# Starting the moving operands of the rounded products 60 bytes into a group of 64 bytes, in a two-block transformer kernel

## What is computed

```python
for i in range(2):                                   # first block
    h = h + 0.5 * swiglu(rms_norm(h, g_ffn1[i]), ffn1_w_in[i], ffn1_w_out[i])   # 1024 -> 2*2816 -> 1024
    hn = rms_norm(h, g_mix[i])
    h = h + (mla_mixer(hn, ...) if i == 0 else fox_mixer(hn, ...))              # two kinds of attention
    h = h + 0.5 * swiglu(rms_norm(h, g_ffn2[i]), ffn2_w_in[i], ffn2_w_out[i])
    gate = sigmoid(rms_norm(h, g_ple[i]) @ ple_w_gate[i])
    h = h + gate * (p[i] @ ple_w_proj[i])
# second block
proj = rms_norm(x) @ w_in                            # 1024 -> 3592
x = x + concat([short_conv_mixer(...), gated_deltanet(...)]) @ w_out
x = x + hier_moe(rms_norm(x))                        # 32 experts, 2 of them per token, inner width 512
return rms_norm(x)
```

## Time and profile before

| | |
|---|---|
| time, median of 3 runs | 1735.52 us (1734.45 to 1735.61) |
| the profiled execution | 1735.63 us, of which the span from first to last instruction is 1733.8 us |
| TensorE busy | 94% of the span, 10376 matmuls |
| VectorE, ScalarE, GpSimd busy | 57%, 35%, 3% |
| mean granted TensorE clock | 0.987 |
| DMA | 415.65 MB, 240 GB/s over the span |

### The profile page before, as it was taken

One profiled execution on the slowest core, in us unless ns is written; L12 is line 12 of the kernel. 1 busy time (PEld: TensorE's weight loads), 2 busy tenths in 40 slices (PEclk: granted clock), 3 DMA queues, 4 the chain that ended last, 5 costly groups with the idle time before them and its releaser, 6 DMA issues.

```text
span 1733.8 us, 25871 instructions
## 1 busy us (share of the span) xinstructions
PE 1631.1 (94%) x10376; PEld 1300.8 (75%) x10376; DVE 987.8 (57%) x1660; ACT 611.2 (35%) x809; POOL 54.3 (3%) x82
## 2 busy tenths in 40 slices
PE   6999999999999999999999999999989788778877
PEld 6999857899998999888899999999854344334333
DVE  6787655687766877865487785788331111111112
ACT  5333346433335333365543334553421000000001
POOL 3000005000000000001200000000000000000000
PEclk9999999999999999999999999999989999999999
DMA  6555441454554455444155555332599999999996
GB/s 267 191 191 185 183 182 74 182 182 181 184 223 176 182 188 191 184 165 182 66 190 187 191 192 202 139 128 92 222 376 426 426 428 427 428 428 427 428 428 268
DMA packets 49240, 415.65 MB, mean 240 GB/s; under 512 B 5616, under 2 KB 5648, under 8 KB 7824
## 3 DMA queue, kind: packets, MB, share of 16 engines
q1 hardware_dynamic: 49104, 414.61, 60.7%
q10 hardware_dynamic: 64, 0.03, 0.0%
HBM read 413.54 MB, written 1.05 MB: 239 GB/s over the span
## 4 chain that ended last, share of the span: by engine, by line
PE 75%; DMA 18%; DVE 3%; ACT 2%; issue 1%; SPq 0%; POOL 0%; DVEq 0%; ACTq 0%
PE bank L546 67%; DMA sb_moe_ring<-experts 18%; PE bank L1240 6%; DVE sb_ring_lo L2001 1%; ACT sb_high L1514 1%; PE bank L735 0%; PE bank L824 0%; DMA sb_h<-xT 0%; SPq L471 0%; ACT sb_high_first L1514 0%; DVE sb_nmax L2134 0%; DVE sb_x_parts L2030 0%; ACT sb_expg L1614 0%; PE bank L944 0%; ACT L1471 0%
## 5 line engine op out<-in xcount | busy, mean ns | idle before, releaser
L2001 DVE TENSOR_TENSOR sb_ring_lo<-sb_ring,sb_high 128x2304 fp32r<-128x2304 f32 (+4 forms) x180 | 352.0, 1957 | 132.4 <-ACT sb_high L1514 131.9
L546 PE MATMUL bank<-sb_x_parts,sb_high 128*128 128x512 f32 (+1 forms) x1792 | 407.0, 366 | 0.2
L546 PEld LDWEIGHTS bank<-sb_x_parts,sb_high 128*128 128x128 f32 x1792 | 317.7, 189 | 49.3 <-DVE sb_ring_lo L2001 0.5
L1514 ACT ACTIVATE sb_high<-sb_ring 128x3072 fp32r<-128x3072 f32 x100 | 275.7, 2757 | 147.2 <-PE bank L546 119.6
L546 PE MATMUL bank<-sb_x_parts,sb_ring_lo 128*128 128x256 f32 x1632 | 257.9, 284 | 0.0
L546 PEld LDWEIGHTS bank<-sb_x_parts,sb_ring_lo 128*128 128x128 f32 x1632 | 228.5, 192 | 6.7
L546 PE MATMUL bank<-sb_act_hi,sb_ring_lo 128*128 128x256 f32 x704 | 199.2, 283 | 0.0
L546 PE MATMUL bank<-sb_act_hi,sb_high 128*128 128x256 f32 x680 | 192.6, 283 | 2.0 <-DVE sb_ring_lo L2001 1.5
L546 PE MATMUL bank<-sb_act_lo,sb_high 128*128 128x256 f32 x680 | 192.4, 283 | 0.0
L1240 PE MATMUL bank<-sb_moe_ring,sb_act 128*32 128x512 f32 x512 | 130.1, 655 | 41.2 <-DMA sb_moe_ring<-experts 41.1
L1556 ACT ACTIVATE sb_expg<-sb_gate_r 128x256 f32<-128x256 f32 x88 | 36.9, 419 | 339.3 <-DVE sb_gate_r L2064 339.2
(11 more groups left out here) (385 smaller groups left out, 1893.9 us busy)
## 6 DMA issues: line engine op xcount, KB each, us to landing
sb_ring<-weights SPq DMA_DIRECT2D x133, 1536.0 KB, 6.5
sb_moe_ring<-experts SPq DMA_DIRECT2D x185, 1024.0 KB, 21.1
sb_qk<-experts SPq DMA_DIRECT2D x4, 1024.0 KB, 15.0
sb_moe_ring<-experts SPq DMA_DIRECT2D x8, 256.0 KB, 17.2
sb_h<-xT SPq DMA_DIRECT2D x2, 512.0 KB, 7.7
sb_ring<-weights SPq DMA_DIRECT2D x2, 512.0 KB, 8.5
sb_oT<-experts SPq DMA_DIRECT2D x1, 1024.0 KB, 15.4
sb_pin<-pT SPq DMA_DIRECT2D x1, 512.0 KB, 18.1
```

The lines of the kernel that those rows point to most:

```text
L546: ins = nc.tensor.matmul(o, l, r, start=start, stop=stop, skip_group_check=True)
L1514: nc.scalar.activation(high_of(n)[:, lo * P:hi * P], ring[:, n % RING, lo * P:hi * P], ACT.Copy).then_inc(done, 1)
L2001: return V.tensor_tensor(ring_lo[:, n % RING, cols], ring[:, n % RING, cols], high_of(n)[:, cols].bitcast(F32), ALU.subtract)
```

## The change

The three tensors whose slices move through the array in rounded products get 16 elements (64 bytes) more, and the operands begin at element 15 of them, 60 bytes behind a multiple of 64. The operand's first group of 64 bytes then holds one element of it, and a run of 256 columns touches 17 groups instead of 16. `act` and `act_lo` share their place, so `act` is shifted alike. To keep the same things from overlapping, 16 elements stand behind `hn`, and several tensors are made in another order: `params` and the narrow columns (`gq`, `eps_col`, `peak`) stand first, `qk`, `v_tok` and `oT` ahead of `h`, `act_hi` behind `sq`. Every tensor other than the shifted views still begins at a multiple of 64 bytes (the narrow columns aside, which are columns of one tensor now).

Each engine has the same instructions in the same order as before; only addresses and strides differ. The shifted operands are moving ones in the rounded products named above. They are stationary ones in `fox_qkv` and at the gates (`x_parts`), and in the experts' down product (`act`). The written side moves too: ScalarE's `x_hi` and VectorE's `x_lo`, `act_hi`, `act_lo` and `act` are written to shifted places.

```diff
+LINE = 16
+INSIDE = 15
...
+        def inside(flat, shape):
+
+            n = math.prod(shape[1:])
+            names = "abc"[:len(shape) - 1]
+            dims = {a: shape[1 + i] for i, a in enumerate(names)}
+            return flat[:, INSIDE:INSIDE + n].rearrange(f"p ({' '.join(names)}) -> p {' '.join(names)}", **dims)
...
-        sb("below_ring", [P, 32])
+        params = sb("params", [P, NPAR])
+        narrow = sb("narrow", [P, 16])
+        gq, eps_col, peak = narrow[:, 0:4], narrow[:, 4:5], narrow[:, 5:6].bitcast(I32)
...
-        act_hi = sb("act_hi", [P, 2, T], F32R)
+        qk = sb("qk", [P, 2 * H, T])
+        qT, kT = qk[:, 0:H, :], qk[:, H:2 * H, :]
+        v_tok = sb("v_tok", [P, 2, D])
+        oT = sb("oT", [P, KD, T])
         h = sb("h", [P, KD, T])
-        x_parts = rounded_view("x_parts", [P, 2, KD, T])
+        x_parts = inside(rounded_view("x_parts", [P, 2 * KD * T + LINE]), [P, 2, KD, T])
         x_hi, x_lo = x_parts[:, 0, :, :], x_parts[:, 1, :, :]
         hn = sb("hn", [P, KD, T])
+        sb("behind_hn", [P, LINE])
         sq = sb("sq", [P, KD, T])
+        act_hi = inside(sb("act_hi", [P, 2 * T + LINE], F32R), [P, 2, T])
...
-        act_lo = rounded_view("act_lo", [P, 2, T])
-        act = sb("act", [P, 2, T])
...
+        act_lo = inside(rounded_view("act_lo", [P, 2 * T + LINE]), [P, 2, T])
+        act = inside(sb("act", [P, 2 * T + LINE]), [P, 2, T])
```

More of the change, by code:

```diff
@@ L7 @@
 from contextlib import ExitStack
+import math
 import numpy as np
@@ L262, in two_block_kernel @@
         route = sqh[:, :, :, :].rearrange("p a b t -> p (a b t)")[:, 0:2 * 352].rearrange("p (c n) -> p c n", c=2)
[L263 to L266, removed]
         posi = v_tok[:, 0, 0:2].bitcast(I32)
```

## The result

The changed kernel takes 1726.36 us (median of 6 runs, 1724.46 to 1727.27), the kernel before 1735.57 us beside it (6 runs, 1734.45 to 1736.29). The ratio is 0.9946, with a 95% interval of 0.9935 to 0.9956: 9.2 us less, a fifth of the 48.6 us of the forecast. The first rows are the page of the kernel after: busy time by engine, then the chain, against the earlier trace rows.

The account below looks back on a forecast made before the run. TensorE was taken as the bound up to about 1250 us, then the experts' transfers. Gains of 15.1 us (512 columns) and 33.5 us (256 columns), together 48.6, took 1735.6 to 1687.0 us; the range was 1672 to 1740 us.

Parts of the forecast that it names:

- What bounds the kernel: Whole kernel: TensorE bounds it up to about 1250 us, then the experts' transfers, whose start moves rigidly with TensorE.
- That 13.3 ns is a first group of 16 elements at half rate: Rounded matmuls: the 13.3 ns beyond their columns is the first 64-byte group arriving at 0.83 ns per element.
- 512 columns, -10.7 ns each, -15.1 us: 1408 rounded matmuls with shifted moving operands: 226.7 to 216.0 ns each, 15.1 us less.
- 256 columns, -8 ns each, -33.5 us: 4192 rounded matmuls with shifted moving operands: about 8 of the 10.7 ns can be had, 33.5 us less.
- The floor of the weights' load, 112 ns: 256-column rounded matmuls: weight loads alone hold each to about 112 ns, so only about 8 ns can be gained.
- The new order of tensors, put at nothing: Tensor addresses: moved by whole groups of 64 bytes, with no row giving a price; counted as nothing.
- A shifted stationary operand, put at nothing: Loads in fox_qkv and its gates: at worst 13.3 ns on 384 loads, 5 us; counted as nothing because covered.
- Nothing else takes over: Feed-forward chunk: at 7.96 us it still covers VectorE's 6.71 and ScalarE's 3.19 us; the ring needs 198 GB/s.
- half (b): Rival: weights already set 256 columns' 120 ns, only 512 columns gain; 1720.4 us; chance 0.17 shared with half (a).
- half (a): Rival: first group gains, 17th costs 6.7 ns; 114 and 227.5 ns, 1712.3 us; chance 0.17 shared with half (b).
- Slower: Rival: every run needs 17 whole groups and the array waits; 46.8 us more, 1782.3 us; chance 0.19.
- nothing: Rival: the 13.3 ns is a fixed price of a rounded matmul wherever its operand lies; 1735.5 us; chance 0.13.

Follow-up runs that it names:

- e5: Matmul streams without the network, operands shifted one 64-byte group at a time, from elements 0 and 15; 256 columns from element 0 took 117.8 to 120.0 ns.
- e6: Matmul streams without the network, moving operand and weights in each of four 64-byte groups, all 16 pairs; 256 columns took 113.3 to 120.0 ns.
- e11: Matmul streams without the network: two runs in different groups, the network's sequence, operands walking over tiles; moving group 0 with weights group 1 took 117.8 or 113.3 ns.
- e4: Matmul streams without the network, 32 matmuls each, varying start element, widths and type; rounded 256 columns with full weights took 116.9 to 120.0 ns.
- e9: Matmul streams without the network: alternating places, narrow weights, 2-byte and plain float32 operands; alternating 256-column streams averaged 117.8 to 118.8 ns.
- e1: Changed kernel with every operand back at element 0 of its group, new tensor order and spare elements kept; 1730.26 us, ratio 0.9969.
- e7: Kernel before with the new tensor order, no offset, and x_parts, act_hi, act_lo three groups past a multiple of four; 1718.12 us, ratio 0.9904.
- e10: Kernel before with x_parts two groups past a multiple of four, other rounded operands at a multiple, new order, no offset; 1739.94 us, ratio 1.0022.

## Why the prediction was off

The direction was right, and 1726.4 lies in the range; the forecast of 1687.0 itself was 39 us too low. By its steps:

- **What bounds the kernel: right.** TensorE's distances moved by 2 to 7 ns, and the end moved with them in every run, in both directions.
- **That 13.3 ns is a first group of 16 elements at half rate: wrong, and this is the step that failed.** It took a match of two numbers for a mechanism. That the time still fell, and lies in the range, is luck in part: the range reached up to no change at all, and over half of the gain came from the groups. With one element in the first group the distance became 116 to 117.5 ns, not 112, and 230, not 216. What stands in its place (e5, e6): the extra is set by how the groups of moving operand and weights lie to each other modulo four, between 6.7 and 13.3 ns at 256 columns and between 13.3 and 20 at 512 from element 0, and at one difference by what ran before as well (e11); 13.3 is what group 0 against group 0 gives for both. The rows had a warning: the first matmuls of a 512-column run are slower than the settled 226.7 of the earlier trace rows (the mean is 228.1), which a fixed extra on each matmul doesn't make.
- **512 columns, -10.7 ns each, -15.1 us: wrong in sign.** +2.0 ns, +2.8 us. In the kernel before they stood at their best place.
- **256 columns, -8 ns each, -33.5 us: right in sign, over twice too large.** -3.7 and -2.4 ns, -12.8 us. The floor of the weights' load, 112 ns from the earlier trace rows, was right: e5 has 111.4 to 111.9 for streams of 144 to 224 columns, and no rounded stream of 256 columns went below 113.3. The plain rows were misread, without effect on the sum: in e4 and e9 a plain float32 matmul shows as two records, so the 215.8 ns of the earlier trace rows are half a matmul.
- **The new order of tensors, put at nothing for want of a row: wrong.** Alone it gave 5.1 us (e1), more than half of the result. A term without a row should have been bounded from both sides and not been set to zero; by e7 and e10 placing alone is worth from -17 to +4 us here.
- **A shifted stationary operand, put at nothing: wrong in kind, small in size.** Its matmuls in `fox_qkv` became 2.4 ns longer in the mean, 0.6 us over 264 of them, inside the 5 us that it was allowed at worst. The cover didn't hide it.
- **Nothing else takes over: right.** VectorE has 6.72 of the chunk's 8.35 us, plain float32 stands at 216.0, and the experts' transfers still take 24.5 us a quad: in the chain of after

```profile
1628.85 24.50 DMA sb_moe_ring<-experts
```

- **The rivals.** By the time half (b), 1720.4 us, was nearest, but it had the 256-column distances stay and the 512-column ones shrink, and the reverse happened. By the signs of the distances it was half (a), with 114 and 227.5 ns, but 1712.3 us; its mechanism (a 17th group's price) doesn't give e1 or e7, where no operand touches a 17th group. "Slower" asked for 127 and 240 ns, "nothing" (1735.5 us) for 120 and 226.7. None of them had the groups' places. The line-crossing rule of the Trainium skill ("SBUF — State Buffer", section "Specifications (TRN2)": lines of 16 bytes, each crossing pays) was held against the change. The runs don't bear it out as a cost that a rounded moving operand shows: a run of 256 from element 15 touches one more such line than one from element 0, and took 115.6 to 117.8 ns where those from element 0 took 113.3 to 120.0 (weights in group 0, e6), and 116.7 to 120.0 against 117.8 to 120.0 in e5; and the period found is 256 bytes.

Open are the mechanism behind the table (that the reads of the moving operand and of the next weights meet in the same part of the memory is argued from the period and from the narrow weights, not shown), what chooses between 113.3 and 117.8, and why 512 columns want the difference 0 and 256 the difference 3. Not tried: `high` in group 3 with `ring_lo` in group 0 and `x_parts` in group 3, which by the table has 226.7 ns for the 512-column products and 113.3 (or the other rhythm's 117.8) for those against `ring_lo`, at the price of mixed pairs in `down`.

## What to carry to other kernels

When a matmul's distance in the trace exceeds its columns by a neat number, vary one thing in a small kernel before a change is built on what the number looks like. With rounded operands, try where moving operand and weights begin, modulo 256 bytes: it costs a spare tensor of 64 to 192 bytes and moved this kernel between 1718 and 1740 us. And treat any new order of tensors as a change that can have a price, to be measured on its own beside the edit that it was made for.

## What the runs showed of the hardware

From element 0, a matmul of rounded operands at the granted clock of 1.00 took 113.3 to 120.0 ns for 256 columns and 226.7 to 233.3 for 512 (e5, e6), with a period of 256 bytes in the address of either operand, where 2-byte operands took 109.2 and 215.8 at every place (e9). At one difference of places its distance depends on what ran before it as well: 117.7 and then 113.7 ns over the same operands (e11). Moving the operands by 192 bytes gave up to 6.7 ns on 256 columns and 17.2 us on this kernel (e7). A start inside a group, at element 15, narrows the differences with the weights in group 0 (115.6 to 117.8, and 230.0; e6), but took 116.7 to 120.0 with the weights in group 2 (e5), where one stream from element 1 took 122.5.
